# One 1 MB transfer in place of two of 512 KB for each quarter of a weight chunk in the first feed-forward phase

## The reference

```python
h2 = modulate(rmsnorm(x, norm_mlp_g[l]), shift2, scale2)      # (512, 2048)
y = jnp.square(jax.nn.relu(h2 @ w_ff1[l])) @ w_ff2[l]         # 2048 -> 8192 -> 2048
x = x + gate2 * y
```

## Time and profile before

| | |
|---|---|
| median of 3 runs | 2241.84 us (2240.45 to 2247.23) |
| the profiled execution: time | 2241.16 us |
| its span in the profile | 2239.4 us |
| PE busy | 2182.1 us, 97% of the span |
| PE weight loads busy | 1926.1 us, 86% |
| DVE busy | 1779.0 us, 79% |
| ACT busy | 1033.4 us, 46% |
| POOL busy | 326.4 us, 15% |

### The profile page before, as it was taken

The page is one execution under the profiler, slowest core; times in us unless marked ns, Lnnn a source line. Parts: engine busy times, 40 slices in busy tenths (PEclk is TensorE's granted clock), DMA queues, the critical chain, the costliest instruction groups (busy, mean ns, idle before and its releaser), DMA issues.

```text
span 2239.4 us, 31645 instructions
## 1 busy us (share of the span) xinstructions
PE 2182.1 (97%) x12452; PEld 1926.1 (86%) x12452; DVE 1779.0 (79%) x1945; ACT 1033.4 (46%) x1371; POOL 326.4 (15%) x183
## 2 busy tenths in 40 slices
PE   6999999999999999999999999999999999999999
PEld 5888888888887878889999999999978888888887
DVE  5876876775645577499889898999998888888886
ACT  5435544533355222265666565656633333333341
POOL 2004344342421344320000000000000000000000
PEclk9999999999999999999999999999999999999999
DMA  9966355455636599325756657567866766666642
GB/s 346 342 216 227 120 195 182 136 198 185 222 137 249 199 326 330 100 85 206 264 190 231 232 206 254 198 223 258 293 227 232 236 216 230 221 210 223 210 147 76
DMA packets 261329, 480.16 MB, mean 214 GB/s; under 512 B 18874, under 2 KB 105404, under 8 KB 258368
## 3 DMA queue, kind: packets, MB, share of 16 engines
q1 hardware_dynamic: 208576, 342.89, 44.8%
q10 hardware_dynamic: 52608, 135.28, 16.3%
HBM read 389.48 MB, written 88.63 MB: 214 GB/s over the span
## 4 chain that ended last, share of the span: by engine, by line
PE 86%; DVE 8%; issue 2%; ACT 1%; DMA 1%; POOL 1%; SPq 1%; ACTq 0%; DVEq 0%; POOLq 0%
PE ps L954 10%; PE ps L955 10%; PE ps L956 10%; PE ps L1451 9%; PE ps L1452 9%; PE ps L1453 9%; PE ps L1495 8%; PE ps L1496 8%; PE ps L1497 8%; DVE wlo L2898 1%; PE ps L988 1%; PE ps L1015 1%; DMA araw<-in_w_ada 1%; PE ps L1244 1%; DVE acc L2313 1%
## 5 line engine op out<-in xcount | busy, mean ns | idle before, releaser
L1451 PE MATMUL ps<-hc,whi 128*128 128x256 f32 x1680 | 477.9, 284 | 5.0 <-DVE wlo L2898 5.0
L1453 PE MATMUL ps<-hc,wlo 128*128 128x256 f32 x1680 | 477.4, 284 | 0.0
L1452 PE MATMUL ps<-hc,whi 128*128 128x256 f32 x1680 | 477.3, 284 | 0.0
L499 POOL TENSOR_TENSOR wlo<-wraw,whi 128x1024 fp32r<-128x1024 f32 (+3 forms) x116 | 291.0, 2520 | 476.1 <-ACT whi L494 436.0
L1495 PE MATMUL ps<-whi,ab 128*128 128x512 f32 x840 | 327.3, 390 | 2.9 <-DVE yacc L2983 2.0
L1451 PEld LDWEIGHTS ps<-hc,whi 128*128 128x128 f32 x1680 | 324.6, 193 | 5.6 <-DVE wlo L2898 5.5
L1496 PE MATMUL ps<-wlo,ab 128*128 128x512 f32 x840 | 326.8, 389 | 0.0
L1497 PE MATMUL ps<-whi,ab 128*128 128x512 f32 x840 | 326.8, 389 | 0.0
L1452 PEld LDWEIGHTS ps<-hc,whi 128*128 128x128 f32 x1680 | 324.5, 193 | 0.0
L1453 PEld LDWEIGHTS ps<-hc,wlo 128*128 128x128 f32 x1680 | 324.5, 193 | 0.0
L2011 ACT ACTIVATE whi<-st 128x1024 fp32r<-128x1024 f32 x180 | 191.0, 1061 | 264.4 <-PE ps L1497 139.9
(11 more groups left out here) (361 smaller groups left out, 3962.4 us busy)
## 6 DMA issues: line engine op xcount, KB each, us to landing
wraw<-in_w_ff SPq DMA_DIRECT2D x128, 512.0 KB, 6.9
st<-in_w_ff SPq DMA_DIRECT2D x120, 512.0 KB, 7.7
araw<-in_w_ada SPq DMA_DIRECT2D x112, 512.0 KB, 6.5
a_d<-ring ACTq DMA_DIRECT2D x109, 512.0 KB, 5.6
ab<-a_d ACTq DMA_DIRECT2D x105, 512.0 KB, 4.4
wraw<-in_w_in SPq DMA_DIRECT2D x72, 512.0 KB, 5.9
arawx<-in_w_ada SPq DMA_DIRECT2D x48, 512.0 KB, 4.5
wraw<-in_w_out SPq DMA_DIRECT2D x32, 512.0 KB, 7.4
```

The costliest lines, as they stand in the source:

```text
L499: pool.tensor_tensor(wlo[:, slot, 0:kb, 0:cols], wraw[:, slot, 0:kb, 0:cols], whi[:, slot, 0:kb, 0:cols].bitcast(F), ALU.subtract).then_in ...
L1451: pe.matmul(dst, w[0][:, c], hi, start=new, stop=False, skip_group_check=True)
L1452: pe.matmul(dst, w[0][:, c], lo, start=False, stop=False, skip_group_check=True)
L1453: ins = pe.matmul(dst, w[1][:, c], hi, start=False, stop=t == 3, skip_group_check=True)
```

## The change

For groups 0 to 14 a quarter is now loaded by one transfer of both halves. It is issued after the waits of both halves have passed, and signals one semaphore, `st_in[r][0]`. Consumers of either half now wait for that one. `uses_of` and `sem_of` count the semaphore's uses; from group 15 on there are again two transfers and two semaphores. Nothing else moves.

```diff
+def sem_of(g, i):
+    return place_of(g, i) if g >= GROUPS_A else 0
...
-def uses_of(g):
+def uses_of(g, i):
+
+    if sem_of(g, i):
+        return g - GROUPS_A
     return g + 1 if g <= GROUPS_A else g
...
         def piece_load(g, r, blocks=(0, 1)):
 
+            k, s = PIECES[r]
             for i in blocks[:blocks_of(g)]:
                 if g == 0 and r < 2:
                     sp.wait_ge(lo_ready, N_FF + 4 + 2 * r + i + 1)
...
-                k, s = PIECES[r]
-                if g < GROUPS_A:
-                    kt, f = 8 * k + 4 * i, CH * (g + 1) + 256 * s
-                    src = w_ff13[:, kt:kt + 4, f:f + 256]
-                    dst = piece(r, place_of(g, i)).rearrange("p a n -> p (a n)").rearrange("p (k c) -> p k c", k=4)
-                else:
+                if g >= GROUPS_A:
                     kt, f = CT * chunks_of(g)[i] + KB * k, 512 * ((g - GROUPS_A) % 2 + 2 * s)
-                    src, dst = w_ff23[:, kt:kt + KB, f:f + 512], piece(r, place_of(g, i))
-                sp.dma_start(dst, src).then_inc(st_in[r][place_of(g, i)], 16)
+                    sp.dma_start(piece(r, place_of(g, i)), w_ff23[:, kt:kt + KB, f:f + 512]
+                                 ).then_inc(st_in[r][place_of(g, i)], 16)
+            if g < GROUPS_A:
+                f = CH * (g + 1) + 256 * s
+                dst = (wraw if r < 2 else st2)[:, 2 * (r % 2):2 * (r % 2) + 2, :, :]
+                sp.dma_start(dst.rearrange("p i a n -> p (i a n)").rearrange("p (k c) -> p k c", k=8),
+                             w_ff13[:, 8 * k:8 * k + 8, f:f + 256]).then_inc(st_in[r][0], 16)
...
-                    act.wait_ge(st_in[WEIGHTS_AT[q]][place_of(g, i)], ST_0 + 16 * uses_of(g))
+                    act.wait_ge(st_in[WEIGHTS_AT[q]][sem_of(g, i)], ST_0 + 16 * uses_of(g, i))
...
-                    dve.wait_ge(st_in[r][j], ST_0 + 16 * uses_of(g))
+                    dve.wait_ge(st_in[r][sem_of(g, i)], ST_0 + 16 * uses_of(g, i))
...
-                dve.wait_ge(st_in[3][j], ST_0 + 16 * uses_of(g))
+                dve.wait_ge(st_in[3][sem_of(g, i)], ST_0 + 16 * uses_of(g, i))
```

## The result

| | before | changed |
|---|---|---|
| median | 2239.99 us (6 runs, 2233.89 to 2247.23) | 2253.97 us (6 runs, 2251.35 to 2261.72) |
| ratio to before, 95% interval | | 1.0065 [1.0048, 1.0082] |
| profiled execution: time, span | 2241.16, 2239.4 us | 2251.35, 2249.6 us |

The change makes the kernel slower by 0.65%, about 14 us. In two later sets of runs it came out at 1.0062 and 1.0063. My 2242.3 us with a range up to 2248 was wrong.

A forecast was written before the change was run, and what follows sets the result against it. PE was taken to bound the kernel, never stopping in groups 1 to 14; 0 + 0.35 (group 1's stop) + 0.1 (group 0) = 0.45, say 0.5 us, on the 2241.84 us median gave 2242.3 us, range 2239 to 2248.

The forecast's parts named there:

- A rule to batch more: Loads: batch to at least 1 MiB; if each fixed part counted in turn, the change would remove 132 us of DMA time.
- The formula of 2.0 us plus bytes: Each DMA costs about 2.0 us plus bytes over 436 GB/s: two halves 6.4 us, one whole 4.4.
- slower, by late b21: Rival, feed-forward loads: 1 MB in 1 KB packets gets through more slowly than two halves, so D over 2.6 us; 9 in 100.
- The break point of D = 2.6 us: PE at position 2: from this D on the slower rival decides, with stops of 6.5 us in the four tightest groups.
- D: Each group's round of loads: how much later the last landing, b21's, comes; taken as 0.7 us, between 0 and 1.74.
- about 290 GB/s (my estimate for this slow beginning...): Start of group 6's round: rate of the later-starting loads up to 1224, leaving 280 KB missing, 0.7 us at 376 GB/s.
- Both now go at 1221.46: Group 6's b12: both halves issue when the second did before, 1.74 us later than the first did.
- Group 0's term: Group 0: b22's landing for DVE's sum, on the path to PE's 3.1 us wait, costs 0.1 us, between 0 and 1.
- The gate load behind b12 (four groups) ... 0: Four groups: gate load slips by D at most, DVE would wait before the last positions' early-made `wlo`s; cost 0.
- The prediction's own table: PE stops at position 2 per group, from spares of 0.35, 0.7, 1.2, 1.7 and about 3 us: 22 us at D = 4.
- The clock term: PE stops: 0.35 us should leave the clock alone; a 1.4 us stop costs at most 1.7 us, half the long one's price.
- three signs that would prove the prediction wrong: b21 over 11.5 us from issue in group 6, PE's `wlo` waits over 10 us in the phase, DMA engines not busy throughout.

The follow-up runs named there:

- e3: Kernel before, but both 512 KB halves issued late and on one semaphore, so the changed kernel in all but transfer size: 2247.15 us, 1.0033 of before.
- a2: The changed kernel run again, beside the fourth set: 2255.60 us against 2239.96 for the kernel before, 1.0063.
- a1: The changed kernel run again, beside the second set: 2253.56 us against 2241.09 for the kernel before, 1.0062.
- e1: Kernel before, two 512 KB halves with a semaphore each, both issued only after the waits of both: 2242.37 us against 2239.63, 1.0009.
- e14: The same kernel as e3 run again, beside a2: 2245.21 us, 1.0022 of the kernel before.
- e6: Kernel before with only group 3's four quarters loaded by 1 MB transfers: 2244.46 us in one execution.
- e12: Changed kernel with each quarter loaded by four 256 KB transfers, issued late, on one semaphore: 2251.72 us against 2242.46 for the kernel before, 1.0040.
- e13: Like e3, but the two 512 KB transfers split the partitions, 64 each with all eight rows: 2352.33 us against 2239.96 for the kernel before, 1.0511.
- e11: Changed kernel with each 1 MB transfer in 512 packets of 2 KB, landing other weights: 2244.48 us against 2242.46 for the kernel before, 1.0006.

## Why the prediction was wrong

**Right.** PE does not stop in groups 1 to 14 before, so nothing could be gained: nothing was. A lone transfer's fixed part is hidden once the queue is full. A rule to batch more, of the Trainium skill's page DMA: Bandwidth & Descriptors, section Bandwidth, would have made this change a gain; e3 against the changed kernel shows the opposite sign here, 0.3 to 0.4%. The formula of 2.0 us plus bytes that the prediction puts beside it stands on the same page, in the section Anatomy of one DMA, as a fit for transfers issued by GpSimd. Its 4.4 us for 1 MB compare with 5.7 here, and its 6.4 us for two halves with 5.1 to 5.4. The rival "slower, by late b21" had the outcome, and half of the mechanism: the 1 MB transfer is slower, but that is 0.3 to 0.4% of the 0.65%. The break point of D = 2.6 us that it names is where the direct D lies in one group.

**The step that failed: "So the last landing slips by D = 0.7 us, between 0 and 1.74."** Group 9's round shows D directly, since its issues come in group 8, where the spare was whole: DVE ended positions 8 and 9 there 4.88 and 6.02 us ahead of PE in both traces. b21 landed 6.24 us before PE's position 2 before, and 3.65 after. D = 2.6 us, and nearly the same in a2 (3.59); a1, whose position 8 had somewhat less spare, gives 2.2 (4.09). Three things lie in it and around it:

1. *The late start is made up less than I reckoned.* b12 was issued 1.84 us later against PE (27.89 to 26.05 us ahead of position 2), near the forecast's 1.74. I reckoned that the slow beginning of the old round had moved little, so that the new one would lack only 280 KB. In e1, which has only the late issue, the median lead over groups 2 to 14 lost 1.2 us, not 0.7, and in group 9 b21 landed 4.20 us before PE, D = 2.0: there nothing was made up. The estimate of "about 290 GB/s (my estimate for this slow beginning...)", with the engines at work until the end behind it, carried this error. e3 and e14 give 2.0 and 2.35 us in group 9. So most of the direct D in this group is the late start, and one group does not resolve what the size adds to it; that shows in the next item and in the leads of all groups. The upper bound of 1.74 was the late start and nothing else, so items 2 and 3 had no place in it.

2. *The transfer of 1 MB is slower.* b12 landed 5.5 to 5.7 us after the first issue as two halves (e14, e3: medians of 14 rounds) and 6.4 to 6.6 as one, and the round ended 0.5 us later. I had kept this as a rival with 9 in 100 and priced a lone one by the 4.2 us of `out<-yacc`. That store row is of another shape; the loads of this phase take 5.7 alone, and 5.5 with packets of 2 KB. The row with the same bytes had neither the shape nor the company.

3. *The next round starts from this one's lateness.* I took the issue times of b12 as fixed by PE ("Both now go at 1221.46"). They come from DVE's `wlo` of positions 8 and 9. With D of 2.6, DVE has no pause left between position 2 and position 9, and reaches position 9 3 us later against PE, so b12 goes 3 us later too: 1225.27 in the profile, where I expected 1221.5. In group 12, the first after group 7 with no spare left, b21 landed 2.39 us before PE instead of 6.47: 4.1 us, and no more only because PE then waits. The round of groups 8 to 12 shows it grow: 4.24, 1.31, 0.92, 0.43, 0.05 of spare. e6 shows that the loop alone does not keep lateness alive; each round has to add its own.

**Group 0's term** was 0.1 us, between 0 and 1, with b22 as one transfer priced at 4.2 us. It took 5.9 (issued 982.74), and DVE had to wait for it before the sum t = 3, where before it had not:

```profile
988.77 1.23 DVE L2880 TENSOR_TENSOR wraw<-st,wraw 128x1024 f32<-128x1024 f32 x1 [0.55 <-DMA st<-in_w_ff]
```

PE's long stop became 3.85 us from 3.11, and a stop of 1.08 us came that before did not have:

```profile
999.12 0.39 PE L1459 MATMUL ps<-hc,whi 128*128 128x256 f32 x1 [3.85 <-DVE wlo L2906]
...
1013.44 0.38 PE L1459 MATMUL ps<-hc,whi 128*128 128x256 f32 x1 [1.08 <-DVE wlo L2906]
```

So the term was 1.8 us of stops. In this trace they did not show in the time, because the granted clock was higher (0.97 against 0.90 from 990 to 1040 us), and group 0 as a whole came out 0.8 us shorter.

**"The gate load behind b12 (four groups) ... 0"** failed too, and in group 7 it was the dearest. Its transfer was issued at 1309.01, behind b12 at 1307.92. DVE waited for it before the sum `acc` that PE's small matmuls read, and `wlo` stood behind it on DVE:

```profile
1316.72 1.28 DVE L3005 SCALAR_TENSOR_TENSOR acc<-acc,silc 128x1024 f32<-128x1024 f32 x1 [0.79 <-DMA acc<-in_w_ada]
```

PE stopped 1.31 us for it (row 1318.06 above). Then the granted clock fell:

```profile
1316.00:1326.00 10.00, 8.69 (x62) 8.49 (x61) 6.49 (x7) 3.30 (x5) 0.00 (x0) 0.83 1.05 384
```

0.83 over 10 us is 3.4 us at the lower of the clock's two levels, 1.2 GHz, which is 1.7 us of work. With the 1.31 us stop that is 3.0 of group 7's 4.1 us; the 0.72 us stop at 1290.55 makes it 3.7.

**The sum of the stops.** The prediction's own table for D = 2.6 gives 6.5 us and for D = 4 more than 20. Measured were 10.2 in the profile. It was right in kind: stops came in groups 1 and 7, where the spare was least, though in groups 6 and 12 to 14 too, where it was not. The table counts each group as if it stood alone. The trace shows two things that it lacks: the 4.1 us that PE lost in group 7 gave group 8 a spare of 4.24, and groups 8 to 11 had no stop; and the spare went down again from round to round.

**The clock term** had its size about right, with 1.7 us as its bound, but it went by the length of a stop, and that does not decide. No stop between 0.6 and 1.5 us at a position 2 lowered the clock (1.47 us at 1046, with 1.00 from 1044 to 1054, first line below); the one in front of the small matmuls did, for 1.7 us. In e14 a stop of only 0.44 us at this same place, at 1317.51, was followed by as much (second line, of e14), while one of 0.43 us in e3 was followed by 1.00.

```profile
1044.00:1054.00 10.00, 8.53 (x72) 8.32 (x71) 10.00 (x11) 7.42 (x12) 0.00 (x0) 1.00 0.20 63
1316.00:1326.00 10.00, 9.56 (x68) 9.35 (x68) 7.11 (x8) 4.03 (x6) 0.00 (x0) 0.83 1.05 374
```

**What the changed profile was to show.** ACT's waits for `st` 70 to 80 us: 89.2. b21 issued near 1233: 1234.55; landing by 1242 to 1244: 1245.76. Of the three signs that would prove the prediction wrong, PE's waits for `wlo` came to 10.8 us (the bound was 10) and b21 took 11.2 us from its issue (11.5): the first just crossed, the second just not, because the loss is partly clock and partly in other waits (for `cb` and `acc`), and 6.9 of the 10.8 us lie in group 0. The DMA engines were busy throughout, as expected.

**What stays open.** Why 1 MB in 1 KB packets gets through a busy queue more slowly than two halves with the same packets. With packets of 2 KB the kernel loses almost nothing, but whether this takes away the cost of merging or outweighs it is not shown, since two halves of 2 KB packets were not run; e12 and e13 did not narrow it down. Also that e11 changes the lead by 1.6 us while a lone transfer gains only 0.2 to 0.4: most of the price exists under load only, and the traces here don't show which resource it is.

## What to carry to other kernels

Before a load is merged or moved, work out the spare in every group from the landing to the engine that must not stop, and then follow the chain round once more: if the next round's issue waits for work that stands behind this landing, lateness is added in every round, and spare that looked ample for one is used up in three or four. Several small delays that each cost 0.1 to 0.2% alone can cost 0.6% together, so a part that measures as nothing on its own isn't free. A transfer's price is to be read from a row with the same packet size and the same load around it, not from one with the same bytes.

## What was not expected of the hardware

One transfer of 1 MB in 1 KB packets was slower than two of 512 KB issued together, alone (5.7 against 5.1 to 5.4 us) and in the round (b12 6.4 to 6.6 against 5.5 to 5.7 us), and a kernel with 1 MB in 2 KB packets lost nearly nothing (1.0006 against 1.0062). A transfer to 64 partitions took 5.4 to 5.5 us where one of the same size to 128 took 3.9, each with its other half issued close behind, and a kernel made of them was 5.1% slower: its DMA engines were as busy in a round (1.06) and moved 272 GB/s instead of 376. The longer stop did not cost more clock: in group 0 PE stopped 3.11 us before and 3.85 us after, and the granted clock from 1000 to 1010 us was 0.74 before and 0.83 after. At one and the same place in group 7, stops of 0.43 and 0.44 us were followed by 1.00 (e3) and 0.83 (e14).
